# A decoder layer on one core: first projection block in another order, with smaller edits in the attention steps and at the end

## The reference

```python
# layer(x, ...), once for the prompt, once for the sample
h = rmsnorm(x, norm_mix_g);  z = h @ w_in            # 1024 x 2576, columns split among the heads
o_gla  = gla_recurrence(...) ; o_pool = pool_mixer(...)
o_diff = diff_attention(dq, k_all, v_all, ...)       # 4 heads, two softmax maps per head, chunk-causal (64)
x = x + concat[o_gla, o_pool, o_diff] @ w_out
x = x + memory_attend(rmsnorm(x), mk, mv)            # 256 memory tokens
x = x + hier_moe(rmsnorm(x))                         # top-1 group of 4, then top-2 of its 4 experts, 16 experts
y = rmsnorm(x, final_norm_g)
```

## Time and profile before

| | us |
|---|---|
| median of 3 runs | 754.03 |
| lowest and highest | 752.98 and 755.75 |
| the profiled execution | 751.27 |
| its span from the first to the last instruction | 749.6 |
| mean granted TensorE clock | 0.966 of full |

### The profile page before, as it was taken

How to read it: one execution, slowest core, us unless ns; L and a number is a source line. 1 busy time by engine, 2 the same in 40 slices (tenths; PEclk the granted TensorE clock), 3 DMA queues, 4 the chain that set the end, 5 groups by cost and what they waited for, 6 DMA issues and landing times.

```text
span 749.6 us, 9426 instructions
## 1 busy us (share of the span) xinstructions
PE 695.4 (93%) x3469; PEld 554.1 (74%) x3469; DVE 522.2 (70%) x697; ACT 424.7 (57%) x602; POOL 139.8 (19%) x157
## 2 busy tenths in 40 slices
PE   5999999999999998889999589999999999999990
PEld 4898887776666675678888468888888888788870
DVE  4436745565567556275466768888999999988873
ACT  5645642245544344173324528888887887778880
POOL 4102840011000101100000220222222222222124
PEclk9999999999999999999999559999999999999996
DMA  8623143212671000130055878999999999999763
GB/s 309 205 106 150 71 161 123 85 56 106 232 292 58 2 1 0 57 141 0 1 208 186 314 284 323 355 374 380 376 383 372 380 372 369 384 366 380 309 218 112
DMA packets 32867, 161.23 MB, mean 215 GB/s; under 512 B 6189, under 2 KB 6523, under 8 KB 18108
## 3 DMA queue, kind: packets, MB, share of 16 engines
q1 hardware_dynamic: 23392, 140.39, 48.9%
q0 software_dynamic: 5344, 10.27, 5.1%
q10 hardware_dynamic: 4092, 10.08, 3.7%
HBM read 149.59 MB, written 20.03 MB: 226 GB/s over the span
## 4 chain that ended last, share of the span: by engine, by line
PE 79%; DVE 11%; ACT 3%; issue 2%; DMA 2%; POOL 1%; SPq 1%; POOLq 0%; ACTq 0%; DVEq 0%
PE pj L2097 44%; PE scores L2097 16%; PE tr_v L2097 12%; DVE wl L1405 4%; PE tr_a L2105 2%; PE scores L2473 2%; PE tr_v L2105 2%; PE tr_a L2502 1%; DMA xT_raw<-in_xT 1%; DVE hid L1405 1%; DVE w_lo L1405 1%; ACT prob L1127 1%; DVE tiny L1656 1%; DMA xg<-h_rows,idx_sb 1%; ACT junk_end L911 1%
## 5 line engine op out<-in xcount | busy, mean ns | idle before, releaser
L1405 DVE TENSOR_TENSOR wl<-moe_raw,wh 128x2048 fp32r<-128x2048 f32 x96 | 218.5, 2290 | 28.1 <-ACT wh L899 27.3
L899 ACT ACTIVATE wh<-moe_raw 128x2048 fp32r<-128x2048 f32 x96 | 182.3, 1919 | 38.8 <-PE pj L2097 12.6
L2097 PE MATMUL pj<-w_hi,xT_hi 128*128 128x512 f32 (+2 forms) x192 | 70.9, 369 | 9.0 <-DVE w_lo L1434 8.4
L745 POOL TENSOR_SCALAR rs<-stat 128x1 f32<-128x1 f32 (+5 forms) x30 | 9.0, 299 | 342.2 <-ACT sq_scr L911 178.0
L2097 PE MATMUL pj<-w_hi,xT_lo 128*128 128x512 f32 (+2 forms) x192 | 69.0, 359 | 0.0
L2097 PE MATMUL pj<-w_lo,xT_hi 128*128 128x512 f32 (+2 forms) x192 | 68.9, 359 | 0.0
L800 POOL DMA_INDIRECT acc_rows<-y,idx_sb x14 | 22.2, 1589 | 207.4 <-ACT y L1329 207.4
L2097 PE MATMUL pj<-wh,xgh 128*128 128x512 f32 x128 | 52.8, 413 | 1.4 <-DVE xgl L1405 1.4
L1434 DVE SCALAR_TENSOR_TENSOR w_lo<-raw,pack_a,w_hi 128x512 fp32r<-128x512 f32 (+2 forms) x64 | 43.7, 744 | 11.5 <-ACT w_hi L943 11.5
L2097 PE MATMUL tr_v<-wh,xgh 128*128 128x512 f32 x128 | 51.1, 399 | 0.0
L2097 PE MATMUL pj<-wh,xgl 128*128 128x512 f32 x128 | 51.0, 398 | 0.0
(11 more groups left out here) (416 smaller groups left out, 1513.5 us busy)
## 6 DMA issues: line engine op xcount, KB each, us to landing
moe_raw<-in_w_exp_gate SPq DMA_DIRECT2D x32, 1024.0 KB, 8.3
moe_raw<-in_w_exp_up SPq DMA_DIRECT2D x32, 1024.0 KB, 9.4
moe_raw<-in_w_exp_down SPq DMA_DIRECT2D x32, 1024.0 KB, 9.4
raw<-in_dense SPq DMA_DIRECT2D x16, 1024.0 KB, 6.0
raw<-in_dense SPq DMA_DIRECT2D x8, 256.0 KB, 6.3
x_rows<-in_x_prompt SPq DMA_DIRECT2D x4, 512.0 KB, 11.8
xw<-in_x_prompt ACTq DMA_DIRECT2D x1, 2048.0 KB, 8.2
h_rows<-h ACTq DMA_DIRECT2D x4, 512.0 KB, 3.7
```

What stands on the lines that cost most here:

```text
L745: link(pool.tensor_scalar(rs[rows, n, cs], stat[rows, n, cs], EPS, None, ALU.add))
L899: act.activation(wh[s4][:, :], moe_raw[n % RING][:, :], ACT.Copy).then_inc(hi_done, 1)
L1405: return dve.tensor_tensor(out, a, b, op)
L2097: return pe.matmul(out, lhsT, rhs, start=start, stop=stop, skip_group_check=True)
```

## The change

- **Block G.** The tiles 0 and 1 are made half by half in turn: rows 0 to 511 for both, then rows 512 to 1023 for both. Tiles 2 and 3 go into two banks of `scores` (`pj_more`), tile 4 again into `pj0`. The transposes of a tile come later: those of tile 0 ahead of tile 3, of 1 ahead of 4, of 2 behind 4, of 3 behind R's tile 0, of 4 behind R's tile 1.
- **Loads at the start.** Of `pack_a` the first 27 columns are loaded alone, the other 316 later (`pack_in`). The x tiles 0, 1 and 2 come in halves, the first half of tile 1 ahead of the fourth weight quarter; `x_rows` come behind x tile 3.
- **Block R.** VectorE makes the low parts of the units 2 and 3 ahead of the copies of tiles 1 and 2 (before: 2 and 3). ScalarE makes the high parts of unit 2 ahead of the reading of tile 2 and those of unit 3 behind it.
- **Attention steps.** In `diff_scores` both maps' products come first and then both masks; `hide_q` and `hide_k` have 64 rows for each map (one of ones, the rest zero) in place of one. The units 16 to 19 are split in pairs of chunks over the steps 1 to 7. In a step with h = 1 the half projection comes ahead of `vrow` by `pdT`. ScalarE reads `memv` one step later.
- **End.** The square of result tile 0 comes ahead of `y_evac`, tile 2's is drawn into the last step, the groups are (0), (1, 2), (3, 4), and VectorE writes tile 0 inside the last step, ahead of `hidden`.

The diff, cut to what the text speaks of:

```diff
-    plan = [((b, t), row_reader(t)) for b, _, _ in IN_BLOCKS[:-1] for t in range(TILES)] + ...
+    plan = [(("G", t), row_reader(t), (0, 1, 2, 3, 0)[t]) for t in range(TILES)]
+    plan += [((b, t), row_reader(t)) for b, _, _ in IN_BLOCKS[1:-1] for t in range(TILES)] + ...
-LATE_SPLIT = {1: 16, 2: 17, 5: 18, 6: 19}
+SPLIT_AHEAD = {6: (18, (2, 3)), 7: (19, (2, 3))}
+SPLIT_BEHIND = {1: (16, (0, 1)), 2: (16, (2, 3)), 3: (17, (0, 1)), 4: (17, (2, 3)), 5: (18, (0, 1)), 6: (19, (0, 1))}
...
-        hide_q = put("hide_q", [CH + 1, P], BF16)
-        hide_k = put("hide_k", [CH + 1, CH], BF16)
+        hide_q = put("hide_q", [P, P], BF16)
+        hide_k = put("hide_k", [P, CH], BF16)
...
+        pj_more = [sc[:, 1024:1536], sc[:, 1536:2048]]
+        pj_of = lambda key: (pj + pj_more)[PJ[key][3]]
...
-        END_COLS = [(0, 2), (2, TILES), (TILES, TILES + 1), (TILES + 1, TILES + 2)]
+        END_COLS = [(0, 1), (1, 3), (3, TILES), (TILES, TILES + 1), (TILES + 1, TILES + 2)]
...
+            for g in range(2):
+                x_half(0, g)
+                for k in range(4):
+                    quarter(g, k)
+                    if (g, k) == (0, 2):
+                        x_half(1, 0)
+            x_half(1, 1)
+            x_half(2, 0)
+            x_half(2, 1)
+            x_load(3)
+            rows_load(0)
...
-            act.dma_start(pack_a[:, :], A["pack_a"]).then_inc(gains_in, 16)
+            act.dma_start(pack_a[:, 0:27], A["pack_a"][:, 0:27]).then_inc(gains_in, 16)
...
+                if s in (2, 4):
+                    mem_out("memv", s // 2 - 1)
+                if s in SPLIT_AHEAD:
+                    w_out_high(*SPLIT_AHEAD[s])
...
-                if s in LATE_SPLIT:
-                    w_high(LATE_SPLIT[s])
+                if s in SPLIT_BEHIND:
+                    w_out_high(*SPLIT_BEHIND[s])
...
+                    end_square(0)
                     y_evac(gsl[:, e - 1:e], 1 - b, 1, 6 * e + 2, None)
-                    end_square(0)
                     end_square(1)
+                    end_square(2)
                     hid_hi(e, b)
...
             for t in range(TILES):
-                if t in (2, 3):
-                    w_low(t)
+                if t in (1, 2):
+                    w_low(t + 1)
                 if t == 4:
                     ...                      # the fold of G's tile 4: four instructions
...
                     split_lo(e, b, 3)
+                    out_tile("end", 0)
                     hidden(e, 6 * e + 4)
...
-            in_block("G", 2, {})
-            in_block("R", 0, {0: lambda: rows_T("G", 4, 2)})
+            for part in range(2):
+                for t in range(2):
+                    pe.wait_ge(xT_lo_done, 2 * part + t + 1)
+                    project(("G", t), t, *x_block(t), BLOCK_UNITS["G"], WIDTH["G"], part)
+            for part in range(2):
+                pe.wait_ge(xT_lo_done, 5 + part)
+                project(("G", 2), 2, *x_block(2), BLOCK_UNITS["G"], WIDTH["G"], part)
+            for t in range(3, TILES):
+                rows_T("G", t - 3, 2)
+                pe.wait_ge(xT_lo_done, t + 4)
+                project(("G", t), t, *x_block(t), BLOCK_UNITS["G"], WIDTH["G"])
+            rows_T("G", 2, 2)
+            in_block("R", 0, {0: lambda: rows_T("G", 3, 2), 1: lambda: rows_T("G", 4, 2)})
...
                         mm(out[:, 0:nk], q, kT[ms, h, 0:nk], True, False)
-                        ins = mm(out[:, nk - CH:nk], hide_q[DH * m:DH * m + 1, :], hide_k[DH * m:DH * m + 1, :], False, True)
...
+                if t < 4:
+                    for m in range(2):
+                        ms = slice(DH * m, DH * m + DH)
+                        ins = mm(half(key)[:, 512 * m + nk - CH:512 * m + nk], hide_q[ms, :], hide_k[ms, :], False, True)
+                    ins.then_inc(sc_full, 1)
...
-                if s == len(STEPS) - 2:
+                early = h == 1 or s == len(STEPS) - 2
+                if early and t:
                     w_out(h // 2, t - 1, h % 2)
+                elif early:
+                    mem_kv("memv", h // 2, h % 2)
```

More of the change, by code:

```diff
@@ L1014, in _ @@
             for t in range(4):
-                if t >= 2:
-                    w_high(t)
+                if t == 2:
+                    w_high(2)
                 n = t
@@ L1359, in _ @@
                 step(e, e % 2, last=e == E - 1)
-            for t in range(2, TILES):
+            for t in range(3, TILES):
                 end_square(t)
@@ L2062, in _ @@
                 step(e, e % 2, last=e == E - 1)
-            for t in range(TILES):
+            for t in range(1, TILES):
                 out_tile("end", t)
@@ L2328, in _ @@
                     mk_T(1)
-                if t and s != len(STEPS) - 2:
+                if t and not early:
                     w_out(h // 2, t - 1, h % 2)
-                elif not t:
+                elif not early:
                     mem_kv("memv", h // 2, h % 2)
```

113 lines of the change are left out of this document (62 added, 51 removed).

## The result

| | before | changed |
|---|---|---|
| median, us | 753.50 (6 runs) | 748.89 (6 runs) |
| lowest and highest | 750.64 and 755.75 | 747.27 and 751.26 |
| the profiled execution, its span | 751.27, 749.6 | 751.26, 749.3 |

The ratio is 0.9942, with a 95% interval from 0.9915 to 0.9969: 4.4 us faster (2.3 to 6.4). Run again later beside the kernel before, the changed kernel had 0.9954 (0.9930 to 0.9977), 3.5 us. The forecast was 4.3 us, 749.7.

The account below looks back on a forecast made before the run. TensorE, busy 93% of the span, was taken as the bound, so savings count only in its work or waits. Terms +2.9 - 5.4 - 1.8 = -4.3 put the profile at 747.0 and the median at 749.7 us, range 745 to 755.5.

Parts of the forecast that it names:

- Two of the signs by which I was to be wrong: After-profile: clock spells in more than two places of the attention, or the last part still waiting for `rs`.
- Term A: Start up to block R: start -1.3, new wait at R +2.7, clock +1.5, together 2.9 us slower.
- The new wait: Ahead of R's tile 1: TensorE idles some 2.7 us until VectorE has folded G's tile 4 out of `pj0`.
- The half clock behind it: Behind the idle time at R: products at the 1.2 GHz clock level, 1.5 us lost.
- The start: From the first product through block G: 0.4 from `pack_a` and 0.9 from the wait for tile 1, 1.3 us gained.
- The wait for tile 1: Block G at 16.79: the wait for tile 1's low part with its restart goes away, 0.9 us gained.
- `pack_a`, 0.4: Start: loading only 27 columns first takes less of the DMA engines; 0.4 us gained, the middle of none and 0.7.
- Term B: Attention steps: shorter scores save 14.8 us, of which 6.2 is kept, less 0.8 for slow clock: 5.4 us gained.
- half a spell more: Attention steps: half a chance of one more spell of slow clock, 0.8 us lost.
- The rival "they don't pay": Attention steps: maps don't run side by side or the gain turns into waits; B -0.5, result 754.6; chance 0.17.
- the slower one: Attention steps: TensorE's longer waits bring six half-clock spells costing 9.0 us; B +2.8, result 757.9; chance 0.06.
- Term C: Last expert step: adds of the last rows come right behind TensorE's last product instead of waiting for ScalarE; 1.8 us gained.

Follow-up runs that it names:

- scores_alone: The kernel before with only the score products changed: both maps side by side, then both masks over 64 rows; ratio to the kernel before 0.9928.
- f_late_vrow: r_fold_first with the half projection behind `vrow` by `pdT` in steps with h = 1 too, as before the change; ratio to the kernel before 0.9849.
- r_fold_first: The changed kernel with VectorE folding block G's tile 4 ahead of its copies of tile 3's transposes; ratio to the kernel before 0.9852, median 742.32 us.
- tail_late: The changed kernel with VectorE writing result tile 0 behind the last expert's `hidden`, not ahead of it; ratio to the kernel before 0.9922.
- wait_filled: The changed kernel with ten unused products of 512 columns put into TensorE's wait ahead of R's tile 1; ratio to the kernel before 0.9938.

## Why the prediction was right, step by step

**The sum.** 4.3 were forecast and 4.4 measured. That they agree to 0.1 is luck: the interval is 4 us wide, the second measurement gave 3.5, and several parts of the terms below didn't come out. By kernels: the start with R costs 2.6, the scores give 5.4, the end gives 1.1 (by the marks to the adds and to the end; no kernel had it alone). That is -3.9, and leaves 0.5 to splits and order, within the scatter.

Two of the signs by which I was to be wrong did appear, though the number held. Half clock was to show in no more than two places of the attention, and both profiles of the changed kernel have it in three; and the last part still waits for `rs`.

**Term A, +2.9: 2.6 (0.7 to 4.5).** The new wait was 2.65 where 2.7 was forecast, at its place, with its releaser and by its chain of offsets. The half clock behind it, 1.5, was there in five of six profiles with 1.3 to 1.5. The start was to gain 1.3. Block R's tile 0 starts at 37.76 and 37.10 in the two profiles with the old block G and at 35.95 to 36.62, 36.25 in the mean, in the twelve with the new: 0.9 to 1.5 less, so the sum was near. Its parts are less clear. The wait for tile 1 is in none of the twelve, but scores_alone, which has the old block G, shows hardly any of it either: its products there start 0.27 and 0.34 apart in place of 0.2275, 0.15 lost in all, where before lost 0.8. The step that failed is `pack_a`, 0.4: no run shows a gain, and the 8.45 of the profile of before, from which I argued, was itself a late start. By the rule of the Trainium skill, "DMA: Bandwidth & Descriptors" (Specifications), that transfers under 512 B are read, modified and written, the 108-byte rows gain near nothing. That none is measured agrees with it, but the runs don't show that the row size is the reason.

**Term B, -5.4: -5.4 for the scores alone.** The price was right to 0.04 us at the three sizes that I read. What was kept, a third, was right in sum and not in its parts: I didn't price the later reading of `memv`, which made a wait of 1.5, and I counted on the half projection in front for `pdT`, which gave nothing (f_late_vrow). The clock was under-priced: I allowed 0.8 for half a spell more, and the two profiles of the changed kernel have 13.6 us at half clock in the stretch, twice the 6.8 of before. Their stretch is only 2.8 shorter than before's, where that of scores_alone, with 6.8, is 6.6 shorter. `xw` was the wait I had named with its lack of slack, and it grew most, from 3.6 to 6.3. The rival "they don't pay" and the slower one have fallen: waits of 1.6 to 2.2 stand at several places, and in the changed kernel's first profile the clock fell at three of them up to 310 us (1.57 at 192.06, 1.90 at 238.31, 2.20 at 299.12), not six. What I held against the slower one was misread, though. I wrote that before only the wait of 2.21 had such an end; the clock also fell to 0.61 from 190 to 192 and to 0.54 from 192 to 194, by a wait of 0.91 at 190.28. Nor does the size of a wait decide it: in r_fold_first the wait of 1.57 at 188.77 has full clock behind it.

**Term C, -1.8: -1.1.** The mechanism was right, the size was off. `out_tile(0)` was to cost 0.2; it puts `hid` 0.9 later, because it waits for GpSimd's norm factor until 724.5. Its first operation took 1.29 us for one column while VectorE was busy; before, the same operation took 0.23 for two columns while VectorE stood idle (that this is the reason isn't shown). With `hid` TensorE's end moved: its last product starts 9.45 behind the mark where it was 8.50, and the adds stand right behind it, as I had put them. Taking the 0.9 away alone gains nothing, since in tail_late, with TensorE's last product at 8.48, the writes of the tiles hold the adds at 9.7. So two things end at the same place, TensorE and VectorE, and I had priced neither: the delay of `hid`, and the norm factors for tiles 3 and 4, for which VectorE still waits 0.93 where I had nothing. There was also a slip of 0.2 in the 1.75: 732.28 and 0.39 make 732.67 and not 732.9, and by that I would have forecast 2.0, farther from the 1.1.

## What to carry to other kernels

When a transpose is moved behind a product, look at what stands behind its reader on the other engine: here four fold instructions, which held the next product's bank, moved with it and cost a wait of 2.65 us and, in five of six profiles, a spell of half clock. Moving the fold, one number, gave more than the whole change had. The shorter scores paid a third of their saving here, where the other engines set the pace of many steps, so price the waits that a shorter product uncovers before its own saving. And single executions of one kernel here lie up to 7.6 us apart (wait_filled), and one attention program took 130.4 to 135.0 us. So read the granted clock of a stretch beside its length before you explain a difference between two profiles by the code.
